# Two weight tiles of the output projection held in spare slots, and the first up-projection slots cast in their place

## The reference, cut to what matters

```
o = concat([rms_norm(o_a, g_out_a), rms_norm(o_b, g_out_b)]) @ w_o     # 1024 x 1024
x = x + gate_a * o
h = rms_norm(x, g_ffn) * (1.0 + scale_f) + shift_f
u = depthwise_conv_centred(h @ w_up, conv_w, conv_b)                   # 1024 x 5632
val, gate = jnp.split(u, 2, axis=-1)
x = x + gate_f * ((silu(gate) * val) @ w_down)
```

## Time and profile before

| | |
|---|---|
| median of 3 runs | 1169.76 us (1169.35 to 1172.54) |
| profiled execution, its own time | 1169.24 us |
| its span, first to last instruction | 1167.5 us |
| PE busy | 1138.8 us (98%) |
| DVE busy | 759.3 us (65%) |
| POOL busy | 591.9 us (51%) |
| ACT busy | 507.7 us (43%) |
| mean granted PE clock | 0.991 of full |

### The profile page before, as it was taken

How to read it: one execution, slowest core, us unless ns; L and a number is a source line. 1 busy time by engine, 2 the same in 40 slices (tenths; PEclk the granted TensorE clock), 3 DMA queues, 4 the chain that set the end, 5 groups by cost and what they waited for, 6 DMA issues and landing times.

```text
span 1167.5 us, 18737 instructions
## 1 busy us (share of the span) xinstructions
PE 1138.8 (98%) x6264; PEld 953.0 (82%) x6264; DVE 759.3 (65%) x1466; ACT 507.7 (43%) x922; POOL 591.9 (51%) x783
## 2 busy tenths in 40 slices
PE   9999999899999999999899999999999999999996
PEld 6897677898888888888789966799888888888886
DVE  6787676767767877788667687746775144412445
ACT  5445765254422344233454567535442244323442
POOL 2483342555555545546766324255555555554552
PEclk7999999999999999999999999999999999999999
DMA  9843610424445444544433111022432322223212
GB/s 345 331 167 123 217 74 19 146 90 162 162 149 208 156 172 180 198 180 173 152 115 120 61 67 37 19 74 90 161 128 93 106 90 99 99 91 107 91 72 73
DMA packets 44123, 151.68 MB, mean 130 GB/s; under 512 B 5138, under 2 KB 7954, under 8 KB 44052
## 3 DMA queue, kind: packets, MB, share of 16 engines
q1 hardware_dynamic: 44052, 150.77, 36.1%
HBM read 148.65 MB, written 2.10 MB: 129 GB/s over the span
## 4 chain that ended last, share of the span: by engine, by line
issue 37%; POOL 29%; PE 19%; POOLq 14%; DMA 1%; DVE 0%; ACT 0%; SPq 0%; DVEq 0%; ACTq 0%
POOL w_lo L601 28%; POOLq L603 10%; PE ps L688 6%; PE ps L694 6%; PE ps L689 6%; POOLq L661 2%; POOLq L659 1%; DMA shift<-shift_slots 1%; POOLq L614 0%; PE ps L820 0%; DVE x L1657 0%; POOLq L599 0%; POOLq L604 0%; ACT w_hi L1244 0%; POOL cg_sg L632 0%
## 5 line engine op out<-in xcount | busy, mean ns | idle before, releaser
L601 POOL TENSOR_TENSOR w_lo<-w_raw,w_hi 128x256 fp32r<-128x256 f32 x712 | 551.9, 806 | 455.2 <-ACT w_hi L1244 436.0
L688 PE MATMUL ps<-h_hi,w_hi 128*128 128x512 f32 (+1 forms) x864 | 316.6, 366 | 2.1 <-POOLq L604 1.9
L689 PE MATMUL ps<-h_lo,w_hi 128*128 128x512 f32 (+1 forms) x864 | 316.0, 366 | 0.0
L694 PE MATMUL ps<-h_hi,w_lo 128*128 128x512 f32 (+1 forms) x864 | 315.9, 366 | 0.0
L1244 ACT CAST w_hi<-w_raw 128x1024 fp32r<-128x1024 f32 x178 | 185.7, 1047 | 196.5 <-PE ps L688 195.9
L2008 DVE SCALAR_TENSOR_TENSOR u_sb<-ps,par,u_sb 128x510 f32<-128x510 f32 x176 | 131.8, 749 | 99.2 <-ACT u_sb L1449 84.9
L688 PEld LDWEIGHTS ps<-h_hi,w_hi 128*128 128x128 f32 x864 | 163.3, 189 | 28.8 <-POOLq L604 2.8
L689 PEld LDWEIGHTS ps<-h_lo,w_hi 128*128 128x128 f32 x864 | 163.3, 189 | 26.2
L694 PEld LDWEIGHTS ps<-h_hi,w_lo 128*128 128x128 f32 x864 | 163.2, 189 | 26.1
L688 PE MATMUL ps<-a_hi,w_hi 128*128 128x512 f32 (+1 forms) x400 | 146.0, 365 | 4.2 <-DVE a_lo L2021 3.0
L689 PE MATMUL ps<-a_lo,w_hi 128*128 128x512 f32 (+1 forms) x400 | 145.4, 363 | 0.0
(11 more groups left out here) (181 smaller groups left out, 1504.8 us busy)
## 6 DMA issues: line engine op xcount, KB each, us to landing
w_raw<-w_slots SPq DMA_DIRECT2D x178, 512.0 KB, 3.5
ada_raw<-ada_slots SPq DMA_DIRECT2D x88, 512.0 KB, 4.1
shift<-shift_slots SPq DMA_DIRECT2D x8, 512.0 KB, 13.8
x_tok<-x_rows SPq DMA_DIRECT2D x4, 512.0 KB, 9.8
x<-x_t SPq DMA_DIRECT2D x4, 512.0 KB, 14.4
y_t<-x SPq DMA_DIRECT2D x3, 512.0 KB, 2.9
y_t<-x SPq DMA_DIRECT2D x1, 256.0 KB, 3.0
y_t<-x SPq DMA_DIRECT2D x2, 128.0 KB, 2.7
```

The lines of the kernel that those rows point to most:

```text
L601: nc.gpsimd.tensor_tensor(w_lo[:, j, c], w_raw[:, j, c], w_hi[:, j, c].bitcast(F32), ALU.subtract)
L688: hh = mm(out, stat[0], mov[0], start=first, stop=False)
L689: hl = mm(out, stat[0], mov[1], start=False, stop=False)
L694: return mm(out, stat[1], mov[0], start=False, stop=last)
```

## The change

Two spare slots are laid over memory of the attention: `spare_hi` over `prob`, `spare_lo` over `prob_t`. WO4 and WO5, the fifth and sixth tile, have their high and low parts there and no longer in the ring (`parts_of`). Their raw slots are used as before.

- ACT casts both right after the four casts of `output_hi` for e = 4 to 7 (`spare_cast`), without waiting for `slot_free`.
- POOL forms their low parts after its last `add_squares`, and after it has waited for the attention's last outputs (`lo_spare`).
- ACT's loop over the first four squares casts WO6, WO7, UP0 and UP1 in place of WO4, WO5, WO6 and WO7. UP0 and UP1 lie at the ring places that WO4 and WO5 no longer take, and wait for a release four counts earlier (`early_hi`).
- In ACT's `norm` of the channel mixer, of the four casts two are left: UP2 at the second place, where UP1 stood, and UP3 at the fourth.

The diff without the memory constants' surroundings:

```diff
+SPARE = 2
+S_SPARE = S_WO + RING
...
+        spare_hi = put("spare_hi", [P, SPARE, SLOT], F32R, at=at_att)
+        spare_lo = put("spare_lo", [P, SPARE, SLOT], F32R, at=at_att + 8192)
         prob = put("prob", [P, 2, 4, SEQ], at=at_att)
         prob_t = put("prob_t", [P, 2, 2, 2, SEQ], at=at_att + 8192)
...
+        def parts_of(n):
+
+            e = n % SLOTS - S_SPARE
+            if 0 <= e < SPARE:
+                return spare_hi[:, e, :], spare_lo[:, e, :]
+            return w_hi[:, n % RING, :], w_lo[:, n % RING, :]
...
+            def lo_spare(n):
+
+                hi, lo = parts_of(n)
+                pool.wait_ge(hi_done, n + 1)
+                for q in range(4):
+                    c = slice(q * SLOT // 4, (q + 1) * SLOT // 4)
+                    nc.gpsimd.tensor_tensor(lo[:, c], w_raw[:, n % RING, c], hi[:, c].bitcast(F32), ALU.subtract)
+                nc.gpsimd.drain()
+                pool.sem_inc(raw_free, 1)
+                pool.sem_inc(split_done, 1)
...
-                lo_slots(L * SLOTS + S_WO + 4, L * SLOTS + SLOTS)
+                pool.wait_ge(o_done, NP * (L + 1))
+                for n in range(L * SLOTS + S_SPARE, L * SLOTS + S_SPARE + SPARE):
+                    lo_spare(n)
+                lo_slots(L * SLOTS + S_SPARE + SPARE, L * SLOTS + SLOTS)
...
-                j = slot(L, S_WO + m)
+                slot(L, S_WO + m)
+                w = parts_of(L * SLOTS + S_WO + m)
...
-            def norm(n, L, s_next):
+            def norm(n, L, slots):
...
-                split_hi(L, s_next)
+                next_hi(0)
...
-                split_hi(L, s_next + 1)
+                next_hi(1)
...
-                split_hi(L, s_next + 2)
+                next_hi(2)
...
-                split_hi(L, s_next + 3)
+                next_hi(3)
...
+            def spare_cast(L, e):
+
+                n = L * SLOTS + S_SPARE + e
+                act.wait_ge(raw_landed[n % RING], 16 * (n // RING + 1))
+                nc.scalar.copy(parts_of(n)[0], w_raw[:, n % RING, :]).then_inc(hi_done, 1)
+
+            def early_hi(L, s):
+
+                n = L * SLOTS + s
+                act.wait_ge(slot_free, n + 1 - RING)
+                act.wait_ge(raw_landed[n % RING], 16 * (n // RING + 1))
+                nc.scalar.copy(w_hi[:, n % RING, :], w_raw[:, n % RING, :]).then_inc(hi_done, 1)
...
+                for e in range(SPARE):
+                    spare_cast(L, e)
                 group_roots(L, 2)
...
                 for e in range(N_UPD - 4):
-                    if e < TAIL:
-                        split_hi(L, S_WO + 4 + e)
+                    if e < TAIL - SPARE:
+                        split_hi(L, S_SPARE + SPARE + e)
+                    elif e < TAIL:
+                        early_hi(L, S_UP[0] + e - TAIL + SPARE)
                     square(2 * L + 1, e)
-                norm(2 * L + 1, L, S_WO + KD)
+                norm(2 * L + 1, L, (None, S_UP[0] + 2, None, S_UP[0] + 3))
```

7 lines of the change are left out of this document (5 added, 2 removed).

## The result

The changed kernel takes 1175.1 us (median of 8 runs, 1172.7 to 1178.5) where the kernel before took 1170.7 beside it (8 runs, 1169.4 to 1172.5): the ratio is 1.0038, with an interval of 1.0027 to 1.0050. That is 4.4 us slower, inside the range of the prediction and 1.1 us more than its sum. The interval excludes 1, so the loss is small but real.

The account below looks back on a forecast made before the run. PE, busy 98% of the span, was taken as the bound, with waits for POOL and low clock in layer 0. Late sums + 2.4, clock + 1.7, up-projection - 0.8 gave + 3.3 us on 1169.76: 1173.0 us, range 1167.0 to 1176.0.

Parts of the forecast that it names:

- Spare slots, at nothing: ACT's two casts fit its idle time, POOL forms WO4 and WO5 early, PE's waits for POOL go; cost nothing.
- Square 0 added 3.6 us later: Layer 0: square 0 stands behind WO6's cast, so DVE adds it at 205.9, not 202.27, idle until then.
- Waits of 3.2 us at the fourth half tile and about 5 at the sums: Layer 0: PE waits 3.2 us for the bank update 4 empties, then about 5 us at `norm_sums`.
- So the whole list moves: Layer 0: DVE has no slack from 202.27 to 223.9, so all its work shifts by 3.6 us.
- Late sums, + 2.4 (2.1 to 2.7): Layer 0: PE passes `norm_sums` at 229.4 to 230.0, not 227.28, including 0 to 0.6 us of POOL contention.
- The clock, + 1.7: Layer 0: low clock behind `norm_sums` after PE stands still, 1.7 us on the path; bounds nothing to twice that.
- The norm and the up-projection, - 0.4 a layer: Norm of both layers: PE waits less for UP slots; 0.4 us won a layer, 0.8 for two (0 to 2.2).
- Layer 1 loses nothing among the half tiles: Layer 1: same late square, but no modulation between tiles, so update 4 at about 773 precedes need at 776.44.
- Nothing later should take it back: After 250 us PE stays the bound and what waits for it moves along, so the + 3.3 us sum stands.
- Clock stays high: Rival: late squares in layer 0 but no low clock, + 2.4 - 0.8, 1171.4 us; chance 0.17.
- Dearer: Rival: low clock twice as long, later `h_lo` in both layers, or sums 2.7 us late; 1175.9 us; chance 0.18.
- DVE catches up: Rival: DVE regains 3.0 us in layer 0 if POOL finishes before about 215; 1166.7 to 1168.1 us; chance 0.10.

Follow-up runs that it names:

- e14: Changed kernel with 18 unread matmuls on PE ahead of layer 0's sequence 0 sums and UP2's cast one place later: 1172.1 us, ratio 1.0015.
- e9: Changed kernel with squares 0, 1, 3 ahead of their casts, 22 unread matmuls ahead of layer 0's sequence 0 sums, UP2's cast one place later: ratio 1.0000.
- e2: Kernel before, no spare slots, with ACT casting WO4, WO5 and WO6 ahead of square 0, so only the squares are late: 1173.2 us, ratio 1.0025.
- e3: Changed kernel with 18 unread matmuls on PE ahead of the sums of sequence 0 in layer 0: ratio 1.0029.
- e8: Changed kernel with squares 0, 1, 3 ahead of their casts and 22 unread matmuls on PE ahead of layer 0's sequence 0 sums: 1172.5 us, ratio 1.0027.
- e4: Changed kernel with UP2's cast one place later in ACT's norm, nothing else: 1178.1 us, ratio 1.0053.
- e1: Changed kernel with squares 0 and 1 ahead of the casts of WO6 and WO7, square 3 ahead of UP1's: 1174.4 us, ratio 1.0039.
- e7: Changed kernel with DVE's eight modulation pieces beside layer 0's half tiles cut from 1024 to 64 columns, the rest left out: 1168.4 us, ratio 0.9986.
- e13: Changed kernel, late squares kept, with three modulation pieces moved ahead of the norm: 1170.8 us, ratio 1.0002.
- e12: Changed kernel with squares 0, 1, 3 ahead of their casts, UP2's cast one place later, three modulation pieces ahead of the norm: 1165.9 us, ratio 0.9960.
- e6: Kernel before with DVE's eight modulation pieces beside layer 0's half tiles cut from 1024 to 64 columns, the rest left out: 1165.4 us, ratio 0.9961.
- e11: Kernel before, no spare slots, with three modulation pieces moved ahead of the norm: 1168.9 us, ratio 0.9992.

## Why the prediction was right, and where its sizes were off

It said 1173.0 us, 3.3 more than before; the measurement says 4.4 more (3.2 to 5.9, from the interval). What it named as the place where the case is decided is the place, and every sign that it listed for layer 0 is in the trace. The size fits less well. Put on the 1169.76 us from which it started, the ratio gives 1174.2 us, near the upper edge of the forecast's own 1171.8 to 1174.5. And two errors partly cancel in it: the late sums came 0.5 us smaller than forecast, the norm 1.3 us larger.

- **Spare slots, at nothing.** Right. The casts stood in ACT's idle time (1.99 us for both), POOL was done with both low parts at 196.2 of its trace, some 12 us before PE began WO4's first half tile (the cast that waits for it starts at 208.52), and PE's waits for POOL at WO6 and WO7 are gone.
- **Square 0 added 3.6 us later.** Right: 205.75 for 202.27, 3.5 us, with 3.68 us of standing still released by ACT. Undone alone, with the clock held up, it is worth 2.4 us at the roots (e14 to e9: 232.56 to 230.20) and 1.8 us in the ratios.
- **Waits of 3.2 us at the fourth half tile and about 5 at the sums.** 2.58, 0.44 at the fifth, and 4.71. "So the whole list moves" by 3.6 us was too much: update 4 came 2.9 us later than before (lined up), because two additions took 0.80 and 0.69 us for 1.06 and 1.03. DVE's last addition began 2.7 us later, for 2.9. And that this is all owed to square 0 was not so: read beside e2, 1.1 us of it come with POOL's two more slots beside DVE.
- **Late sums, + 2.4 (2.1 to 2.7).** 1.9. The contention of POOL with the last piece and addition, for which I had added up to 0.6, did not come: they took 1.23 and 0.43 us again. The step that failed is the overlap: lined up, the piece began at 225.1 and POOL had ended at 224.4. So the 1.4 us that the prediction worked out by the Trainium skill (SBUF — State Buffer, "Who interferes with whom") weren't put to the test there; where the two did meet on one instruction, in the norm, it cost DVE 0.58 us.
- **The clock, + 1.7.** 1.6: 4.92 us from sums to roots, for 3.31. e3 confirms the cause: with PE at work there it is 3.41, and e8, e9 and e14 have 3.42 to 3.43 in the same way. The size is one draw of several, and that it met the 1.7 so well is luck: the same instructions gave 2.7 in e4 (6.03 us). On the Trainium skill's rule (TensorE: Matmul & The Clock Gate, "HAM oscillation — how this bites in real kernels") the prediction wrote that both new waits would be dearer. The traces agree in part: the changed kernel's shows one low stretch for the two, e4's one behind each, and in e3 and e14, where PE was kept at work ahead of the sums, the bank's wait alone was followed by one.
- **The norm and the up-projection, - 0.4 a layer.** In this trace the term is wrong in its sign: root to root takes 13.05 us in layer 0 and 13.04 in layer 1, for 12.79, so + 0.5 us in place of - 0.8. The waits were about as forecast (ACT waited 1.25 us at UP2's cast, for 1.4). What the sum left out is one instruction. DVE's `h_lo` at 243.03 runs while POOL forms the last quarter of UP2's low part and takes 1.06 us, so DVE ended its squares 10.06 us behind the roots (245.49 + 0.42 - 235.85) and not 9.8. The rows are DVE and POOL of the changed kernel, then the same two instructions in e3, whose code is the same there:

```profile
243.03 1.06 DVE L1634 SCALAR_TENSOR_TENSOR h_lo<-xn,mod,h_hi 128x256 fp32r<-128x256 f32 x1
```

```profile
240.62 3.19 POOL L612 TENSOR_TENSOR w_lo<-w_raw,w_hi 128x256 fp32r<-128x256 f32 x4 [14.45 <-ACT w_hi L1275]
```

```profile
241.32 0.48 DVE L1636 SCALAR_TENSOR_TENSOR h_lo<-xn,mod,h_hi 128x256 fp32r<-128x256 f32 x1
```

```profile
238.90 3.50 POOL L612 TENSOR_TENSOR w_lo<-w_raw,w_hi 128x256 fp32r<-128x256 f32 x4 [12.95 <-ACT w_hi L1277]
```

  In e3 POOL gives way (3.50 us for its slot), DVE is done 9.5 us behind the roots, PE waits 0.43 us and not 0.97, and root to root is 12.47. Six traces have UP2's cast at this place (changed, e1, e3, e7, e8, e13), two layers each. In five of the twelve stretches DVE takes 1.06 or 1.07 us, POOL 3.19 or 3.20, and root to root is 13.04 or 13.05; in the other seven it is 0.48 us, 3.49 or 3.50, and 12.45 to 12.48. So the forecast's - 0.4 a layer is what the seven show (- 0.3), and the profiled execution drew the other case twice. Why DVE gives way in one execution and POOL in another stays open. With the cast one place later (e4, e9, e12, e14) all eight stretches take 12.09 to 12.12 us: a gain of 0.7 a layer, of the 1.1 that I had as the bound, was there to be had. (For both layers together the bound was 0.2 us too high: before the change layer 1 has no wait of 0.21 us.)
- **Layer 1 loses nothing among the half tiles.** Right: no wait of PE there.
- **"Nothing later should take it back."** Not quite. The profiled execution is 5.4 us longer than that of before, lined up, and 3.7 us of it are there by the second roots, 0.25 more come in layer 1. Behind 582 the clock is low for 3.4 us after a wait of 2.98 us for `a_lo`, which stood in the kernel before too, with the clock at 1.00 behind it:

```profile
582.38 0.47 PE L713 MATMUL ps<-a_hi,w_hi 128*128 128x512 f32 x1 [2.98 <-DVE a_lo L2069]
```

```profile
577.00:580.00 3.00, 3.00 (x13) 2.49 (x14) 1.75 (x4) 1.83 (x2) 0.70 (x2) 1.00 0.17 59
```

```profile
583.00:586.00 3.00, 3.00 (x9) 2.32 (x8) 1.75 (x4) 1.81 (x2) 0.93 (x2) 0.50 0.05 20
```

The first fence is the changed kernel's wait, the second the stretch behind the same wait before, the third the one after. A low stretch behind this wait is in twelve of the fourteen traces of this case, with spare slots and without (e6, e11), and missing in those of the kernel before and of e2. So I don't count it to the change; which executions have it was not tested.

**The rivals.** "Clock stays high" is out in the changed kernel, and is what e3 made by hand. "Dearer", at 1175.9 us, is nearer to the measured median of 1175.1 than the forecast is (by the ratio, 1174.2, the forecast is nearer), but not by its terms: in the profiled execution the clock was low for 3.4 us and not for twice that, and the late sums stayed below 2.7. Only its third, more time in the norm in both layers, came in part (0.25 us each). "DVE catches up" is out: it wanted POOL done before about 215, and POOL was done at 224.4; DVE had made up 0.6 us by update 4, and not 3.0. Even with pieces a sixteenth as long the sums came 1.8 us later with the change (e7) than without it (e6). What the prediction did not see is the other half of the case: that undoing the late squares would not have saved the change. Before, POOL and DVE held PE nearly to the same time, POOL with two waits early in the stretch, while DVE was done 1.0 us ahead of the sums. With POOL's waits gone PE's idle time doesn't go, it gathers in front of the sums, and there it costs a low clock on the path as well.

## What to carry to other kernels

If two engines hold a third to nearly the same time, taking away the waits for one only moves the idle time to the place where the other ends. Add up the list of the second engine before, and first move work out of it into its own idle time; here three pieces moved, with the squares first and one cast a place later, turned + 0.4% into - 0.4%. In a loop that casts a weight and then does work that others wait for, look at what the cast waits for: work that is ready goes ahead of a wait, never behind it. And of idle time it matters where it stands and in how many pieces: right ahead of the work that everything waits for it cost 1.6 to 2.7 us of clock on top (changed, e1, e4). Last, ask what an engine that is now earlier will stand beside: POOL's two more slots next to DVE's list cost DVE some 1.1 us, as far as two traces side by side can tell.

## What the runs showed of the hardware

- The start-up differs by up to 4.6 us between executions, with the same instructions (mark at 176.26 to 180.84 us in fourteen profiled executions); the runs of one kernel spread over as much. An effect of 1 to 2 us is read better between two marks of the trace than from medians of six runs: e8 and e9 differ by 3.2 us in the ratio and by 0.4 in the lined-up span.
- The same instructions get a different clock from execution to execution. 4.71 us of stillness were followed by 3.4 us at the low level in the changed kernel; e4, with the same code up to the sums, had 3.86 us and 6.8 us at the low level; e1 had 5.67 and 6.8. The wait of 2.9 to 3.0 us for `a_lo` (ending between 571 and 584) was followed by a stretch of low clock in twelve executions and by none in two.
- When a DVE instruction and a POOL quarter meet, either can be the one that pays, with the same code: 1.06 us for 0.48 on DVE, or 3.50 for 3.19 on POOL's slot, five times and seven times in twelve stretches.
- DVE's pieces and POOL's low parts slow each other, and for POOL it decides: a slot of four quarters took 2.82 us with DVE idle for half of it and no piece beside it, and 4.26 to 4.61 beside the pieces (these two rows are of the changed kernel), while a piece grew only from 1.23 to 1.56 us.

```profile
193.35 2.82 POOL L624 TENSOR_TENSOR spare_lo<-w_raw,spare_hi 128x256 fp32r<-128x256 f32 x4 [0.26 <-issue]
...
221.56 4.61 POOL L612 TENSOR_TENSOR w_lo<-w_raw,w_hi 128x256 fp32r<-128x256 f32 x4 [0.32 <-issue]
```
